# A third 2x2 block product in the SwiGLU gate/up units of a hybrid decoder layer, with the pieces of a unit put in another order

## The reference

```python
h = rmsnorm(x, g_ffn[i])
x = x + (jax.nn.silu(h @ w_ffn_gate[i]) * (h @ w_ffn_up[i])) @ w_ffn_down[i]
```

## Time and profile before

| | us |
|---|---|
| median of 3 runs | 1466.37 |
| the profiled execution | 1466.9 |
| its span, first to last instruction | 1465.1 |
| PE busy | 1448.6 |
| DVE busy | 1013.6 |
| ACT busy | 726.2 |

### The profile page before, as it was taken

The page is one execution under the profiler, slowest core; times in us unless marked ns, Lnnn a source line. Parts: engine busy times, 40 slices in busy tenths (PEclk is TensorE's granted clock), DMA queues, the critical chain, the costliest instruction groups (busy, mean ns, idle before and its releaser), DMA issues.

```text
span 1465.1 us, 18813 instructions
## 1 busy us (share of the span) xinstructions
PE 1448.6 (99%) x6786; PEld 1212.0 (83%) x6786; DVE 1013.6 (69%) x1231; ACT 726.2 (50%) x908; POOL 61.6 (4%) x90
## 2 busy tenths in 40 slices
PE   8999999999999999999999999999999999999997
PEld 7888888888888888888888888888888888888886
DVE  7976776667655567676888888545679888656654
ACT  7544444544454455456555455433445555345544
POOL 4021001100111000000000000000000000000000
PEclk9999999999999999999999999999999999999999
DMA  7666565556655567677666667655666677666751
GB/s 211 206 182 172 173 201 172 172 173 191 184 163 167 169 219 226 210 249 243 215 215 214 198 203 249 212 189 170 193 197 207 207 231 243 207 209 219 241 187 58
DMA packets 183680, 291.15 MB, mean 199 GB/s; under 512 B 18808, under 2 KB 67888, under 8 KB 183344
## 3 DMA queue, kind: packets, MB, share of 16 engines
q1 hardware_dynamic: 173936, 281.52, 61.2%
q10 hardware_dynamic: 9664, 8.57, 1.9%
HBM read 275.87 MB, written 2.11 MB: 190 GB/s over the span
## 4 chain that ended last, share of the span: by engine, by line
PE 94%; DVE 2%; DMA 1%; POOL 1%; ACT 1%; issue 1%; ACTq 0%; DVEq 0%; POOLq 0%
PE acc L1690 26%; PE acc L1666 16%; PE acc L1695 13%; PE acc L1671 8%; PE acc L1545 8%; PE side L1690 6%; PE acc L1554 4%; PE side L1695 3%; PE side L1666 1%; PE side L1821 1%; PE side L1818 1%; PE side L1819 1%; PE acc L1821 1%; PE acc L1818 1%; PE acc L1819 1%; PE side L1671 1%
## 5 line engine op out<-in xcount | busy, mean ns | idle before, releaser
L1268 DVE TENSOR_TENSOR l_ring<-w_ring,h_ring 128x1024 fp32r<-128x1024 f32 x320 | 379.3, 1220 | 153.9 <-ACT h_ring L738 137.6
L738 ACT ACTIVATE h_ring<-w_ring 128x1024 fp32r<-128x1024 f32 x280 | 290.3, 1056 | 275.7 <-PE acc L1695 139.8
L935 DVE TENSOR_TENSOR ls<-ws,hs 128x1024 fp32r<-128x1024 f32 x216 | 262.2, 1236 | 159.8 <-ACT hs L521 155.8
L521 ACT ACTIVATE hs<-ws 128x1024 fp32r<-128x1024 f32 x216 | 225.3, 1057 | 269.4 <-PE acc L1671 101.6
L1690 PE MATMUL acc<-h_ring,xg 128*128 128x512 f32 x1312 | 324.0, 389 | 0.0
L1690 PEld LDWEIGHTS acc<-h_ring,xg 128*128 128x128 f32 x1312 | 246.2, 188 | 51.1
L1695 PE MATMUL acc<-l_ring,xg 128*128 128x512 f32 x656 | 175.3, 389 | 0.0
L1666 PE MATMUL acc<-hs,hn 128*128 128x512 f32 (+1 forms) x704 | 171.9, 387 | 0.0
L1666 PEld LDWEIGHTS acc<-hs,hn 128*128 128x128 f32 x704 | 127.0, 188 | 24.2
L1695 PEld LDWEIGHTS acc<-l_ring,xg 128*128 128x128 f32 x656 | 123.1, 188 | 25.6
L1545 PE MATMUL acc<-hn,hs 128*128 128x512 f32 x560 | 139.5, 393 | 0.6 <-ACT hs L526 0.3
(11 more groups left out here) (273 smaller groups left out, 1501.6 us busy)
## 6 DMA issues: line engine op xcount, KB each, us to landing
ws<-in_w_in SPq DMA_DIRECT2D x152, 512.0 KB, 4.4
w_ring<-in_w_ffn_gate SPq DMA_DIRECT2D x88, 512.0 KB, 3.8
w_ring<-in_w_ffn_up SPq DMA_DIRECT2D x88, 512.0 KB, 4.8
w_ring<-in_w_ffn_down SPq DMA_DIRECT2D x88, 512.0 KB, 4.4
ws<-in_w_out SPq DMA_DIRECT2D x32, 512.0 KB, 4.8
w_ring<-in_w_ple_gate SPq DMA_DIRECT2D x32, 512.0 KB, 4.4
ws<-in_w_o_b SPq DMA_DIRECT2D x16, 512.0 KB, 4.1
ws<-in_w_o_a SPq DMA_DIRECT2D x16, 512.0 KB, 4.8
```

Source lines behind the costliest of these rows:

```text
L521: act.activation(hs[:, j, :], ws[:, j, :], ACT.Copy).then_inc(h_split, 1)
L738: act.activation(h_ring[:, i % H_SLOTS, :], w_ring[:, j, :], ACT.Copy).then_inc(h_split, 1)
L935: dve.tensor_tensor(ls[:, j, :], ws[:, j, :], hs[:, j, :].bitcast(F32), ALU.subtract).then_inc(l_split, 1)
L1268: dve.tensor_tensor(l_ring[:, j, :], w_ring[:, j, :], h_ring[:, i % H_SLOTS, :].bitcast(F32), ALU.subtract).then_inc(l_split, 1)
```

## The change

`GROUPS` becomes 3: k-tile pairs 0, 1 and 2 of units 1 to 10 go as block products, pairs 3 to 7 as plain pieces. A unit has 22 ring pieces, 16 of them loaded; the groups stand at pieces 2, 8 and 14. The plain pieces of gate (chunks 3 to 7) stand at 0, 1, 6, 7 and 12, that of up chunk 3 at 13, those of up chunks 4 to 7 at 18 to 21. The orders of SP, ACT, DVE and PE are written anew to fit. On ACT the moves and `ff_hi` keep their places by number, behind the highs of pieces 8 and 9; on SP the moves stay behind the load of piece 15; on DVE `ff_low` stands behind `sum_2` of group 1, ahead of `sum_4`, the first sums of group 2 and the lows of group 1. `x_sum`, `s_sum` and `xs` grow by a half, so `e_g` moves to 188 KB and `p_cols` to 108 KB.

```diff
--- before.py
+++ after.py
@@ -70,8 +70,8 @@
 
 W_SLOTS, H_SLOTS = 12, 6
 HALVES = (6, N_FFN - 6)
-GROUPS = 2
-BLOCKS_AT = (2, 10)
+GROUPS = 3
+BLOCKS_AT = (2, 8, 14)
 PLAIN, MIXED = 2 * K_CH, 2 * K_CH + 2 * GROUPS
 T_AT = tuple(at + e for at in BLOCKS_AT for e in (2, 3))
 DOWN_CH = tuple(2 * units for units in HALVES)
@@ -162,10 +162,10 @@
     hn = sb("hn", 48, [KT, 2 * TOK], F32R)
     mixed = sb("mixed", 48, [2, KT, TOK], F32R)
     ff = sb("ff", 48, [2, 4 * HALVES[0], TOK], F32R)
-    x_sum = sb("x_sum", 88, [GROUPS, 2, 2, P])
-    s_sum = sb("s_sum", 92, [4, GROUPS, P])
+    x_sum = sb("x_sum", 84, [GROUPS, 2, 2, P])
+    s_sum = sb("s_sum", 90, [4, GROUPS, P])
     xs = sb("xs", 96, [2, 4, GROUPS, P], F32R)
-    e_g = sb("e_g", 104, [3, WIDE])
+    e_g = sb("e_g", 188, [3, WIDE])
     h_ring = sb("h_ring", 112, [H_SLOTS, CHUNK], F32R)
     w_ring = sb("w_ring", 136, [W_SLOTS, CHUNK])
     l_ring = sb("l_ring", 136, [W_SLOTS, CHUNK], F32R)
@@ -212,7 +212,7 @@
     q_st = sb("q_st", 199.5, [TOK])
     k_st = sb("k_st", 200.5, [TOK])
     v_st = sb("v_st", 201.5, [2, P])
-    p_cols = sb("p_cols", 192, [KT_PLE, 2 * TOK], F32R)
+    p_cols = sb("p_cols", 108, [KT_PLE, 2 * TOK], F32R)
     t_rows = sb("t_rows", 196, [QUADS, 4, 2, QUAD])
     p_tok = sb("p_tok", 200, [2, D_PLE])
     ident = sb("ident", 202.5, [P])
@@ -394,20 +394,22 @@
         def load_unit(u):
 
             i = unit_at(u)
-            load_gate(i, u, 2)
-            load_gate(i + 1, u, 3)
+            load_gate(i, u, 3)
+            load_gate(i + 1, u, 4)
             load_gate(i + 2, u, 0)
             load_up(i + 3, u, 0)
-            for c in range(4, K_CH):
-                load_gate(i + 2 + c, u, c)
-            load_gate(i + 10, u, 1)
-            load_up(i + 11, u, 1)
-            load_up(i + 14, u, 2)
-            load_up(i + 15, u, 3)
+            load_gate(i + 6, u, 5)
+            load_gate(i + 7, u, 6)
+            load_gate(i + 8, u, 1)
+            load_up(i + 9, u, 1)
+            load_gate(i + 12, u, 7)
+            load_up(i + 13, u, 3)
+            load_gate(i + 14, u, 2)
+            load_up(i + 15, u, 2)
             if u != HALVES[0]:
                 move_quads(sp, T_FF + u - 1, 0)
             for c in range(4, K_CH):
-                load_up(i + 12 + c, u, c)
+                load_up(i + 14 + c, u, c)
 
         def load_down(half, n, c):
 
@@ -755,11 +757,15 @@
             act.wait_ge(chunk_used, C_FFN - H_SLOTS + i + 1)
             act.activation(h_ring[:, i % H_SLOTS, :], w_ring[:, i % W_SLOTS, :], ACT.Copy).then_inc(h_split, 1)
 
-        def blocks_high(u, g):
-
-            i, sums = unit_at(u) + BLOCKS_AT[g], 3 * (GROUPS * (u - 1) + g)
+        def raw_high(u, g):
+
+            i = unit_at(u) + BLOCKS_AT[g]
             piece_high(i)
             upper_high(i + 1)
+
+        def summed_high(u, g):
+
+            i, sums = unit_at(u) + BLOCKS_AT[g], 3 * (GROUPS * (u - 1) + g)
             sums_high(i + 2, sums + 1)
             sums_high(i + 3, sums + 3)
 
@@ -790,12 +796,19 @@
             else:
                 piece_highs(unit_at(u + 1), 2)
 
-        def next_blocks(u):
+        def next_raw(u):
 
             if u in (HALVES[0] - 1, N_FFN - 1):
-                piece_highs(unit_at(u) + MIXED + 2, 4)
+                piece_highs(unit_at(u) + MIXED + 2, 2)
             else:
-                blocks_high(u + 1, 0)
+                raw_high(u + 1, 0)
+
+        def next_summed(u):
+
+            if u in (HALVES[0] - 1, N_FFN - 1):
+                piece_highs(unit_at(u) + MIXED + 4, 2)
+            else:
+                summed_high(u + 1, 0)
 
         def ff_unit(u):
 
@@ -803,20 +816,24 @@
             piece_highs(i + 6, 3)
             if u != HALVES[0]:
                 move_quads(act, T_FF + u - 1, 1)
-            piece_high(i + 9)
+            upper_high(i + 9)
             if u != HALVES[0]:
                 ff_hi(u - 1)
-            blocks_high(u, 1)
-            piece_highs(i + 14, MIXED - 14)
-            act.wait_ge(chunk_used, C_FFN + i + 14)
+            summed_high(u, 1)
+            piece_highs(i + 12, 2)
+            raw_high(u, 2)
+            summed_high(u, 2)
+            piece_highs(i + 18, 4)
+            next_highs(u)
+            act.wait_ge(chunk_used, C_FFN + i + 18)
             act.wait_ge(ff_s, u)
             act.activation(e_g[:, 0, :], side[:, 0, :], ACT.Copy).then_inc(e_first, 1)
-            next_highs(u)
+            next_raw(u)
             act.wait_ge(gate_sum, u)
             for b in range(2):
                 ins = act.activation(e_g[:, 2 * b, :], e_g[:, 2 * b, :], ACT.Silu, scale=rms[:, 0, 1, b:b + 1])
             ins.then_inc(ff_silu, 1)
-            next_blocks(u)
+            next_summed(u)
 
         piece_highs(4, 2)
         move_quads(act, T_FF - 1, 1)
@@ -834,7 +851,8 @@
         act.activation(xs[:, 0, :, :, :], s_sum[:, :, :, :], ACT.Copy).then_inc(xs_high, 1)
         piece_highs(14, 2)
         next_highs(0)
-        next_blocks(0)
+        next_raw(0)
+        next_summed(0)
 
         for u in range(1, HALVES[0]):
             ff_unit(u)
@@ -850,7 +868,8 @@
             if n < N_WIDE - 1:
                 piece_highs(i + DOWN_CH[0], H_SLOTS)
         piece_highs(I_REST, 2)
-        blocks_high(HALVES[0], 0)
+        raw_high(HALVES[0], 0)
+        summed_high(HALVES[0], 0)
         for u in range(HALVES[0], N_FFN):
             ff_unit(u)
         for n in range(N_WIDE):
@@ -1358,40 +1377,49 @@
 
             i = unit_at(u)
             last = u in (HALVES[0] - 1, N_FFN - 1)
+            s = i + MIXED
             piece_low(i + 6)
             sums_1_3(u, 1)
             piece_low(i + 7)
             sum_2(u, 1)
-            piece_low(i + 8)
-            sum_4(u, 1)
-            piece_low(i + 9)
             if u != HALVES[0]:
                 ff_low(u - 1)
+            sum_4(u, 1)
+            sums_1_3(u, 2)
             blocks_low(u, 1)
-            piece_lows(i + 13, MIXED - 13)
+            sum_2(u, 2)
+            piece_low(i + 11)
+            sum_4(u, 2)
+            piece_lows(i + 12, 2)
+            blocks_low(u, 2)
+            piece_lows(i + 17, 5)
+            if not last:
+                sums_1_3(u + 1, 0)
+            piece_low(s)
+            if not last:
+                sum_2(u + 1, 0)
+            piece_low(s + 1)
             dve.wait_ge(e_first, u)
             dve.wait_ge(ff_ready, u)
             steps = 2 * (u - 1)
             dve.tensor_tensor(e_g[:, 1, :], e_g[:, 0, :], side[:, 1, :], ALU.add).then_inc(e_step, 1)
             if not last:
-                sums_1_3(u + 1, 0)
+                sum_4(u + 1, 0)
             dve.wait_ge(e_step, steps + 1)
             dve.tensor_tensor(e_g[:, 2, :], e_g[:, 1, :], side[:, 2, :], ALU.add).then_inc(e_step, 1)
             if not last:
-                sum_2(u + 1, 0)
+                dve.wait_ge(t_sum, 3 * (GROUPS * u + 1))
+            piece_low(s + 2)
             dve.wait_ge(e_step, steps + 2)
             dve.tensor_tensor(e_u[:, :, :], e_g[:, 1:3, :], side[:, 3:4, :].broadcast_to([P, 2, WIDE]),
                               ALU.subtract).then_inc(e_ready, 1)
-            s = i + MIXED if last else unit_at(u + 1)
-            piece_low(s)
+            if last:
+                piece_low(s + 3)
+            else:
+                upper_low(s + 3)
             dve.wait_ge(e_ready, u)
             dve.tensor_tensor(e_g[:, 0:3:2, :], e_g[:, 0:3:2, :], acc[:, 2:4, :], ALU.add).then_inc(gate_sum, 1)
-            if last:
-                piece_lows(s + 1, 4)
-            else:
-                sum_4(u + 1, 0)
-                piece_low(s + 1)
-                blocks_low(u + 1, 0)
+            piece_low(s + 4)
             up_result(u)
             piece_low(s + 5)
 
@@ -1860,14 +1888,17 @@
                 pe.wait_ge(x_half, 3)
             else:
                 pe.wait_ge(gate_sum, u - 1)
-            piece_by_token(i, tiles_of_chunk(2), xg, gate_banks, whole, False)
-            piece_by_token(i + 1, tiles_of_chunk(3), xg, gate_banks, going, False)
+            piece_by_token(i, tiles_of_chunk(3), xg, gate_banks, whole, False)
+            piece_by_token(i + 1, tiles_of_chunk(4), xg, gate_banks, going, False)
             block_products(u, 0)
+            piece_by_token(i + 6, tiles_of_chunk(5), xg, gate_banks, going, False)
+            piece_by_token(i + 7, tiles_of_chunk(6), xg, gate_banks, going, False)
+            block_products(u, 1)
+            piece_by_token(i + 12, tiles_of_chunk(7), xg, gate_banks, going, False)
+            piece_by_token(i + 13, tiles_of_chunk(3), xg, up_banks, second, False)
+            block_products(u, 2)
             for c in range(4, K_CH):
-                piece_by_token(i + 2 + c, tiles_of_chunk(c), xg, gate_banks, going, False)
-            block_products(u, 1)
-            for c in range(2, K_CH):
-                piece_by_token(i + 12 + c, tiles_of_chunk(c), xg, up_banks, second if c == 2 else going, c == K_CH - 1)
```

(1 more changed line is left out.)

## The result

The changed kernel takes 1539.75 us, the median of 4 runs (1534.91 to 1544.39), against 1465.83 for the kernel before (now of four runs): 1.0504 times as long, with a 95% interval of 1.0486 to 1.0521. It is slower, as forecast, but by 73.9 us where 40 had been forecast, and it lies outside the range of 1490 to 1530. The profiled execution took 1544.39 us, its span 1542.5 us, 77.4 more than before. It was the slowest of the four, 4.6 us above their median, with the lowest granted clock over the span, 0.973 for 0.976 to 0.979; what follows accounts for this execution.

What follows compares the result with a forecast made beforehand. PE's matmul count was taken as the bound; nine stalls of 5.2 us (46.8) less 6.8 saved gave +40.0, added to the median 1466.4 for 1506.4 us. The range was 1490 to 1530.

Steps and rivals of the forecast that it cites:

- What bounds the kernel: In the FFN units PE never waits, so only the number of matmuls counts; 186 a unit at 0.2267 us.
- the 6.8 us saved: On PE the third group takes 21 matmuls for 24: 0.68 us a unit, ten units, 6.8 us in all.
- Unit 6 keeps its gain: Unit 6 has no ff_low, so its first low is 1 us early and it keeps its 0.68 us.
- The wait that decides: PE waits for group 1's first low, behind ff_low, ff_hi and the quad DMAs: 5.2 us in each of nine units.
- The transposes just ahead of the moves: DVE's transposes end about 6.7 us into the unit for 4.1, still covered by 0.4 us before ACT's moves at 7.1.
- the gate sum just in time: DVE's gate sum, which frees the next unit's banks, is 0.8 us early, so there is no second stall.
- When the quads land: Last quad lands 3.2 us after issue, as before; 1.8 would give 1493, unit 7's offset 1515.
- The clock: Rival: PE's clock falls to 1.2 GHz in stalls, 4.5 us each, +41: 1547, or 1527 in half the units; chance 0.21.
- the first case: The stall as worked out, nine units, with no clock fall; own range 1492 to 1516, chance 0.67.
- DVE as the bound alone: Rival: quads don't matter, DVE's 39.3 us of work plus waits sets units of 41.5 to 42.5: 1460 to 1470; chance 0.05.

Runs made afterwards that it cites:

- x8_all_three: Changed kernel, ff_hi and ff_low behind pieces 12 and 13, next unit's first summed high ahead of gate-sum wait, group 2's first sums behind group 1's lows: 1458.77 us.
- x6: Changed kernel with only the first sums of group 2 on DVE moved behind the lows of group 1: 1525.94 us.
- x9: Kernel before with its two groups, group 1 at piece 8 for piece 10, loads, highs and lows ordered as in the changed kernel: 1527.55 us.
- x1: Changed kernel with only ff_low on DVE moved, from ahead of sum_4 to behind the lows of group 1: 1497.30 us.
- x5: Changed kernel with SP's loads of pieces 14 and 15 behind its quad moves, which still wait for piece 3 to be used: 1519.20 us.
- x2: Changed kernel with ff_hi on ACT and ff_low on DVE both behind pieces 12 and 13: 1474.08 us.
- x3: Changed kernel, ff_hi and ff_low behind pieces 12 and 13, next unit's first summed high on ACT ahead of the gate-sum wait: 1474.39 us.
- x4: Changed kernel with 24 further unwanted matmuls on PE ahead of the third matmul of group 1's first product, in nine units: 1523.34 us.

## Why the prediction was wrong, point by point

- **What bounds the kernel, and the 6.8 us saved**: right. 30 matmuls fewer, 0.227 us each; x8_all_three has units of 41.48 us, and after's -6.8 is needed to close its account.
- **Unit 6 keeps its gain, nine units stop**: right, nine stops, none in unit 6.
- **The wait that decides**: right in place and order. x6 and x9 moved it as its terms say, and x1 removed it, though with other short stops than foretold. The first low ends 3.98 + 1.2 us after ff_hi starts; in unit 3 of after it is 821.34 + 1.22 - 817.37 = 5.19.
- **The transposes just ahead of the moves, the gate sum just in time**: right. DVE's transposes of unit 3 end at 6.7 (806.57), ACT's moves start at 7.09, and no stop stands at a unit's start.
- **When the quads land: the term mis-sized**, the first of two. The prediction took ff_hi at 16.0, with 16.93 as its far end; it was 17.50 in unit 3 and 17.6 on average (16.6 to 18.6), and the stops were 6.7 us on average for 5.2: 60.4 for 46.8, 13.6 us. It had named the loads of 12 to 15 that come close before the quads, and then took the landing of before since "the same queue at the same moment gave it". The queue and its last two loads were the same, the traffic ahead of them was not: the load at 5.6 was still in flight. The last quad took 5.0 us in unit 3 for 3.2. The 6.0 us of the earlier trace rows would have covered that, but the far end of ff_hi was taken from the nine units of before alone. The constant 2.0 us that the prediction cites from the Trainium skill ("DMA: Bandwidth & Descriptors") is given there for transfers issued by GpSimd's path (section "Anatomy of one DMA — SWDGE (gpsimd) path"), and these are issued by ScalarE and SyncE. The 1.9 of x5, where the loads ahead had landed, lies near it, the 3.2 of before and the 5.0 of after do not.
- **The clock: the rival that came true, and the second term.** It stood at 0.21 and was put at nothing in the sum; it cost 23.8 us. The one stop of that length in before was the 4.7 us at the start with a clock of 1.00, and I let that speak against a fall, though it lies at the start of a run and I had said that what PE did ahead of it isn't seen. The rule on half clock after waits between bursts of matmuls (the Trainium skill, "TensorE: Matmul & The Clock Gate", section on HAM oscillation) is borne out by the 0.50 above. The rival's price, 4.5 us a unit by running all 20 remaining matmuls slowly, was too high as well: it is 2.6 on average, since the clock is back before the group ends.
- **The range** ended at 1530 as it took half of the clock's rival and no sum of both misses. The first miss alone would have stayed inside, 1506.4 + 13.6 = 1520.0; the second alone gives 1530.2, at the edge; both give 1543.8, close to the profiled execution's 1544.39, while the median came out lower at 1539.75. The clock's term did not need the late landing: the stops of x9 are 3.9 to 5.7 us, about the 5.2 that was forecast, and all nine lowered the clock, for 17.8 us together. So it belonged to the first case from the start.
- **DVE as the bound alone**: not seen. x8 holds 39.35 us of work in 41.48 with PE never waiting.

## What to carry to other kernels

When work that has a full engine waiting for it is moved forward, list what stands ahead of it in the queue of the engine that prepares it, and ask for each whether it waits for a transfer; a step whose result is needed much later (here ff_low, needed only in the down projection) belongs behind the work that is needed now. Price the landing of a transfer by what is still in flight ahead of it in the new order, also further back than the last issue, and not by its time in the old one. And once a stop of PE of some four microseconds or more is forecast in a stream like this one (all 36 such stops here lowered the clock), the slow matmuls behind it belong in the sum and not among the rivals.

## What the runs showed of the hardware

**Stops and the clock.** The listed stop of PE, and the granted clock in the 8 us behind it:

| kernel | stops, us | clock behind them |
|---|---|---|
| x1_low_later | 34 of 0.2 to 1.7 | 1.00, all |
| x2, x3, x4 | 20 of 0.2 to 1.9, and one of 2.23 | 1.00, all |
| x2_ff_later | 1.98; 2.68 | 0.79; 0.82 |
| x3_first_sum; x4_fill | 3.00; 1.99 | 0.79; 0.79 |
| x5_loads_behind | 9 of 4.2 to 5.5 | 0.64 to 0.80 |
| x9_place_alone | 9 of 3.9 to 5.7 | 0.64 to 0.82 |
| x6_sums_later | 9 of 4.9 to 6.3 | 0.63 to 0.82 |
| after | 9 of 5.6 to 7.6 | 0.61 to 0.79 |

Two stops of 1.98 and 1.99 us lowered the clock and one of 2.23 did not, so length alone does not decide near 2 us. All 36 stops of 3.9 us and more in the last four rows lowered it. By the sum of 8 x (1 - clock) a fall costs 2.0 to 2.1 us on average in x5, x6 and x9 and 2.6 in after. Within after the longest stop (7.58 us, clock 0.70) cost less than one of 5.99 (0.63), so the length of the stop alone does not set the cost.

**Transfers beside each other.** The last of a unit's sixteen quad DMAs (32 KB each), by the loads of 512 KB issued ahead of it, over the nine units; times of issue are from the unit's start:

| kernel | loads issued at, us | last quad, issue to landing, us | ff_hi at, mean, us |
|---|---|---|---|
| before | -2.5, 0.2, 7.0, 7.7 | 2.7 to 4.4 | 16.0 |
| after | 2.9, 5.6, 7.0, 7.7 | 4.1 to 5.7 | 17.6 |
| x9_place_alone | 2.9, 5.6, 7.0, 7.7 | 4.1 to 5.7 | 17.5 |
| x5_loads_behind | 2.9, 5.6 | 1.9, and 3.2 once | 14.2 |

The load issued at 7.7 took 4.8 to 6.6 us in before and 6.2 to 8.2 in after, with sixteen quads issued around it in both; in x3_first_sum DVE went on 9.2 us after its issue in one unit. What differs between before and after is the load at 5.6, two microseconds ahead of it. How much the quads slow the loads no run separates.
